# A 20-slot weight ring that first lends six slots to the attention's tensors, single buffers in the experts, and a new map for the second block

## What is computed

```python
def first_block(...):
    hn = rms_norm(h, mix_norm_g[l])
    proj = jnp.einsum('bld,dp->blp', hn, w_in[l])          # 1024 x 3072
    ...                                                    # attention and convolution
    h = h + jnp.einsum('blm,md->bld', mixed, w_out[l])     # 1024 x 1024
    h = h + expert_choice_ffn(rms_norm(h, ffn_norm_g[l]), w_router[l], w_gate[l], w_up[l], w_down[l])

def expert_choice_ffn(h, w_router, w_gate, w_up, w_down):
    ...
        logits = jnp.einsum('ld,de->le', hs, w_router, preferred_element_type=jnp.float32)
        aff = jax.nn.softmax(logits, axis=-1)
        g, idx = lax.top_k(aff.T, cap)                     # cap = 34
        xg = hs[idx]
        a = jnp.einsum('ecd,edf->ecf', xg, w_gate)         # 16 x 1024 x 2048
        u = jnp.einsum('ecd,edf->ecf', xg, w_up)           # 16 x 1024 x 2048
        y = jnp.einsum('ecf,efd->ecd', jax.nn.silu(a) * u, w_down)   # 16 x 2048 x 1024
        y = y * g[..., None].astype(y.dtype)
        out = jnp.zeros((L, D), y.dtype).at[idx.reshape(-1)].add(y.reshape(-1, D))
```

## Time and profile before

| what | value |
|---|---|
| time, median of 3 runs | 1813.72 us (1812.1 to 1817.64) |
| the profiled execution: time, span | 1817.68 us, 1815.6 us |
| PE, PEld busy | 1546.1 us (85%), 877.3 us (48%) |
| DVE, ACT, POOL busy | 570.1, 365.4, 132.9 us |
| read from memory, mean rate | 509.23 MB, 281 GB/s |

### The profile page before, as it was taken

How to read it: one execution, slowest core, us unless ns; L and a number is a source line. 1 busy time by engine, 2 the same in 40 slices (tenths; PEclk the granted TensorE clock), 3 DMA queues, 4 the chain that set the end, 5 groups by cost and what they waited for, 6 DMA issues and landing times.

```text
span 1815.6 us, 18257 instructions
## 1 busy us (share of the span) xinstructions
PE 1546.1 (85%) x7629; PEld 877.3 (48%) x7629; DVE 570.1 (31%) x982; ACT 365.4 (20%) x662; POOL 132.9 (7%) x137
## 2 busy tenths in 40 slices
PE   7989798787877877878778778699698979979999
PEld 6564433222221322222212222297587779968887
DVE  2353300100100101001001010396675564767843
ACT  1221110000000000000000000255132445445542
POOL 1000000000000000000000000101331160320000
PEclk9999799999999999999999999899898989989999
DMA  9220699999999999999999999553231324545554
GB/s 385 107 93 24 241 416 415 415 419 416 415 415 419 416 415 415 419 415 415 416 419 416 415 416 419 227 163 128 82 105 56 105 79 147 167 140 168 191 194 143
DMA packets 99665, 511.47 MB, mean 282 GB/s; under 512 B 9520, under 2 KB 9776, under 8 KB 64640
## 3 DMA queue, kind: packets, MB, share of 16 engines
q1 hardware_dynamic: 97744, 504.68, 71.2%
q10 hardware_dynamic: 1616, 3.93, 0.6%
q0 software_dynamic: 224, 1.70, 0.3%
HBM read 509.23 MB, written 1.05 MB: 281 GB/s over the span
## 4 chain that ended last, share of the span: by engine, by line
PE 45%; DMA 40%; DVE 9%; ACT 3%; POOL 2%; issue 2%; ACTq 0%; SPq 0%; DVEq 0%; POOLq 0%
DMA sb_ring<-in_w_up 23%; DMA sb_ring<-in_w_gate 15%; PE PS L703 7%; PE PS L1051 6%; PE PS L622 5%; PE PS L430 4%; PE PS L660 4%; PE PS L720 3%; PE PS L739 2%; PE PS L639 2%; PE PS L812 2%; PE PS L532 2%; PE PS L719 1%; DVE sb_wp L1837 1%; DMA sb_ring<-in_w_down 1%
## 5 line engine op out<-in xcount | busy, mean ns | idle before, releaser
L622 PE MATMUL PS<-sb_ring,sb_XG 128*64 128x512 f32 x2048 | 492.6, 606 | 124.9 <-DMA sb_ring<-in_w_up 65.9
L622 PEld LDWEIGHTS PS<-sb_ring,sb_XG 128*64 128x64 f32 x2048 | 129.2, 136 | 482.8 <-DMA sb_ring<-in_w_up 163.6
L1815 DVE TENSOR_TENSOR sb_Hh<-sb_SL,PS 128x512 f32<-128x512 f32 x32 | 20.6, 684 | 831.8 <-PE PS L622 831.8
L660 PE MATMUL PS<-sb_ring,sb_HT 128*64 128x512 f32 x1024 | 234.5, 607 | 30.8 <-DMA sb_ring<-in_w_down 16.2
L1837 DVE TENSOR_TENSOR sb_wp<-sb_raw,sb_wp 128x1024 fp32r<-128x1024 f32 x160 | 201.7, 1263 | 97.2 <-ACT sb_wp L1237 95.7
L703 PE MATMUL PS<-sb_hr,sb_wp 128*128 128x256 f32 x1440 | 190.0, 295 | 8.1 <-ACT sb_wp L1237 5.4
L1237 ACT CAST sb_wp<-sb_raw 128x1024 fp32r<-128x1024 f32 x160 | 167.0, 1046 | 128.6 <-PE PS L1051 56.1
L703 PEld LDWEIGHTS PS<-sb_hr,sb_wp 128*128 128x128 f32 x1440 | 184.7, 202 | 11.8 <-issue 8.2
L660 PEld LDWEIGHTS PS<-sb_ring,sb_HT 128*64 128x64 f32 x1024 | 80.8, 139 | 174.3 <-issue 108.1
L1214 ACT ACTIVATE sb_SL<-PS 128x512 f32<-128x512 f32 x32 | 17.4, 594 | 536.8 <-PE PS L622 536.8
L720 PE MATMUL PS<-sb_hr,sb_wp 128*128 128x512 f32 x256 | 89.9, 404 | 3.4 <-DVE sb_hr L1850 3.4
(11 more groups left out here) (387 smaller groups left out, 1242.4 us busy)
## 6 DMA issues: line engine op xcount, KB each, us to landing
sb_ring<-in_w_gate SPq DMA_DIRECT2D x128, 1024.0 KB, 24.2
sb_ring<-in_w_up SPq DMA_DIRECT2D x128, 1024.0 KB, 25.3
sb_ring<-in_w_down SPq DMA_DIRECT2D x128, 1024.0 KB, 21.0
sb_raw<-in_w SPq DMA_DIRECT2D x160, 512.0 KB, 3.6
sb_ring<-in_w_in SPq DMA_DIRECT2D x12, 1024.0 KB, 15.2
sb_ring<-in_w_out SPq DMA_DIRECT2D x4, 1024.0 KB, 10.0
sb_KW<-in_kw POOLq DMA_DIRECT2D x1, 1403.0 KB, 6.3
sb_H<-in_x ACTq DMA_DIRECT2D x2, 512.0 KB, 5.1
```

The lines of the kernel that those rows point to most:

```text
L622: ins = e.matmul(PS[64 * g:64 * g + 64, b, :], m.XG[:, k, r0:r0 + 64], m.ring[s][:, (2 * g + q) * 512:(2 * g + q) * 512 + 512], start=(k = ...
L660: ins = e.matmul(PS[64 * g:64 * g + 64, b, :], m.HT[:, ex % 2, c % 8, (c // 8) * 64:(c // 8) * 64 + 64], m.ring[s][:, a * 1024 + g * 512:a ...
```

## The change

The ring gets 20 slots. Loads 0 to 15 go through the first 14 of them; slots 14 to 19 hold tensors of the first attention until these are dead. The expert loads then go round all 20 in the order `ROUND`, in which the slots come free:

```diff
-RING = 12
+RING = 20
+IN_SLOTS = 14
+ROUND = tuple(range(2, 12)) + tuple(range(14, 20)) + (12, 13, 0, 1)
+RAW_SLOT, WP_SLOT = 6, 9
-def ring_turn(i):
-    return i % RING, i // RING + 1
+def ring_slot(i):
+    return i % IN_SLOTS if i < 16 else ROUND[(i - 16) % RING]
...
+def last_of(s):
+    last = expert_slot(NE - 1, 23)
+    return max(i for i in range(last - RING + 1, last + 1) if ring_slot(i) == s)
```

What SP waits for ahead of load i (in `sp_program`):

```diff
+    def freed(i):
+        s = ring_slot(i)
+        if i < IN_SLOTS:
+            return []
+        if i < 16:
+            return [used(i - IN_SLOTS)]
+        if i >= 16 + RING:
+            return [used(i - RING)]
+        if s < 2:
+            return [used(IN_SLOTS + s)]
+        if s < IN_SLOTS:
+            return [used(s)]
+        if s < 17:
+            return [("in", "o", 2), ("out", "conv", 11)]
+        if s < 18:
+            return [("in", "oT", 2), ("out", "conv", 11)]
+        return [("in", "wo", 1, 1), ("meta rows",)]
-        if i >= RING:
-            sp.wait_ge(*at(*used(i - RING)))
+        for event in freed(i):
+            sp.wait_ge(*at(*event))
```

**Room for it.** `aT` and `wk` of the top-k lie in `gbc`, and so ACT issues the load of the final gains only after the ranks are turned. In the experts `Y` and `HT` have one buffer, and `Hh` is gone (DVE multiplies within `SL`):

```diff
-                act.wait_ge(*at("out", "gu", ex - 1, q, 1))
+                act.wait_ge(*at("in", "ht", ex - 1, q))
...
-        if ex > 1:
-            act.wait_ge(*at("used", expert_slot(ex - 2, 23)))
-        e.copy(m.HT[:, ex % 2, 0:4, :], PS[:, b, :].rearrange("p (k c) -> p k c", k=4)).then_inc(*mark("act_moe", "out", "ht", ex, 0))
+        if ex > 0:
+            act.wait_ge(*at("used", expert_slot(ex - 1, 23)))
+        e.copy(m.HT[:, 0:4, :], PS[:, b, :].rearrange("p (k c) -> p k c", k=4)).then_inc(*mark("act_moe", "out", "ht", ex, 0))
...
-        if p > 1:
-            act.wait_ge(*at("in", "sc", p - 2, 1, 1))
+        if p > 0:
+            act.wait_ge(*at("in", "sc", p - 1, 1, 1))
```

**The second block's map.** Its tensors are laid anew: `hr` over slots 0 and 1, `raw` over 6 and 7, `KW` over 7 and 8, `wp` over 9 to 12. The first three pieces are split before the last expert's result is copied out:

```diff
 (ACT, in the loop over experts, between the copy to HT and the copies to Y)
+        if ex == NE - 1:
+            for n in range(3):
+                act.wait_ge(*at("used", last_of(WP_SLOT + n)))
+                hi(n)
...
 (ACT, after the second block's norm)
-    hi(0)
+    e.dma_start(m.SW, t["sgw"]).then_inc(*mark("ld_sgw", "sgw", by=16))
     turned("h1", m.sq)
-    hi(1)
-    hi(2)
...
 (DVE, after the last copy to HT)
+    for n in range(3):
+        lo(n)
     scattered(NE // 2 - 1)
...
-    lo(0)
     dve.wait_ge(*at("kw2"))
     turned("h1", m.VW[:, W_N1:W_N1 + 8], m.sq)
-    lo(1)
-    lo(2)
```

`KW` is loaded by SP, behind raw piece 2, and no more by POOL; `SW` by ACT:

```diff
         fetch_raw(raw_turn(n), t["w2"][n], ("lo", n))
+        if n == 2:
+            sp.wait_ge(*at("used", last_of(RAW_SLOT + 1)))
+            sp.wait_ge(*at("used", last_of(RAW_SLOT + 2)))
+            e.dma_start(m.KW, t["kw2"]).then_inc(*mark("ld_kw2", "kw2", by=16))
```

More of the change, by code:

```diff
@@ L252, in take @@
             return v
+        at[0] = ring0 + 2048 * IN_SLOTS
+        self.qraw, self.t1, self.t2 = take("qraw", 2 * L, 2), take("t1", 2 * L, 2), take("t2", 2 * L, 2)
+        self.kT = take("kT", 4 * L, 4)
+        self.qT = take("qT", 4 * L, 4)
+        self.Am, self.AT = take("Am", 2 * L, 2), take("AT", 2 * 3 * 128, 2, 3)
+        self.cv = take("cv", 2 * L, 2)
+        assert at[0] <= ring0 + 17 * 2048
+        at[0] = ring0 + 17 * 2048
+        self.O, self.up = take("O", 3 * 512, 3), take("up", 2 * (L + 2), 2)
+        self.O2 = take("O2", 3 * 512, 3)
+        self.mixT = take("mixT", 8 * L, 8)
+        ar0 = ring0 + 2048 * RING
+        assert at[0] <= ar0
+        at[0] = ar0
         self.XN = take("XN", 3072, 3)
@@ L256, in __init__ @@
         self.junk = take("junk", 1024)
-        self.qraw, self.t1, self.t2 = take("qraw", 2 * L, 2), take("t1", 2 * L, 2), take("t2", 2 * L, 2)
-        self.kT = take("kT", 4 * L, 4)
-        self.qT = take("qT", 4 * L, 4)
         self.V = take("V", 3 * 512, 3)
[L261 to L269, removed]
+        self.Pm = take("Pm", 4 * L, 2, 2)
+        self.cxs = take("cxs", L)
+        self.aT = self.gbc[:, 0:L + 6]
+        self.wk = self.gbc[:, 280:280 + 2 * (L + 6)].rearrange("p (a b) -> p a b", a=2)
         at[0] = ar0
@@ L293, in __init__ @@
         self.BH = hr.rearrange("p q (j c) -> p q j c", j=2)
-        raw0 = ring0 + WR * 2048 + 4096
-        self.raw_over = (raw0 - ring0) // 2048
+        at[0] = ring0 + 4096
+        self.R1, self.R4 = take("R1", 4096), take("R4", 4096)
+        raw0 = at[0]
+        assert raw0 == ring0 + 2048 * RAW_SLOT
         self.raw = [sb(f"raw{r}", raw0 + 1024 * r, 1024) for r in range(RAW)]
-        big0 = at[0] = raw0 + 1024 * RAW
-        self.R1, self.R4 = take("R1", 4096), take("R4", 4096)
+        at[0] = raw0 + 1024 * RAW
+        KW = take("KW", NK2 + NW2)
+        self.KW, self.KT, self.VW = KW, KW[:, 0:NK2], KW[:, NK2:NK2 + NW2]
+        at[0] = ring0 + 2048 * WP_SLOT
+        wp = sb("wp", at[0], WR * 2048, F32R).rearrange("p (w q c) -> p w q c", w=WR, q=2)
+        self.wp_hi, self.wp_lo = [wp[:, w, 0, :] for w in range(WR)], [wp[:, w, 1, :] for w in range(WR)]
+        big0 = at[0] = at[0] + WR * 2048
         self.NN = NN = take("NN", 3072)
@@ L423, in proj @@
     def proj(tile, bank, slot, half):
-        s, turn = ring_turn(slot)
+        s = ring_slot(slot)
         b = room(bank, *tile)
@@ L1199, in act_program, with hi @@
                      accum_out=m.rt[0:n, 4 * ti + 1:4 * ti + 2]).then_inc(*mark("act_out", "out", "lg", ti))
-    for ti in range(3):
-        act.wait_ge(*at("xn2", ti))
+    act.wait_ge(*at("ranks"))
+    act.wait_ge(*at("in", "ranksT"))
     e.dma_start(m.gbc, t["gbc"][1]).then_inc(*mark("ld_gbc", "gbc", 1, by=16))
+    def hi(n):
+        if n < P_END:
+            act.wait_ge(*at("raw", raw_turn(n)))
+            if n >= WR:
+                act.wait_ge(*at(*piece_done(n - WR)))
+            e.copy(m.wp_hi[n % WR], m.raw[raw_turn(n) % RAW]).then_inc(*mark("act_split", "hi", n))
     for c in range(8):
```

91 lines of the change are left out of this document (36 added, 55 removed).

## The result

The changed kernel takes 1796.18 us (median of all 4 executions) where the kernel before took 1814.39 on the same chip; the ratio is 0.9894, 95% interval 0.9872 to 0.9916. One of the four, 1855.01 us at a granted clock of 0.83 over the whole span, is left out of the ratio, and why it was slow isn't known; the other three took 1793.74, 1795.79 and 1796.57, and 1795.79 is their median. The predicted time was 1794.2, the range 1789 to 1800. The profiled execution took 1793.74 us with a span of 1791.5.

What follows compares the result with a forecast made beforehand. The experts' end was taken as set by when the unbroken weight stream starts and the loads still to come. 20.2 + 0.3 - 1.0 = 19.5 us less, from the median 1813.72 to 1794.2 us; range 1789 to 1800.

Steps and rivals of the forecast that it cites:

- The eight slots: Expert weight stream: eight more loads land before it starts at 212.43, each worth 2.526 us; 20.2 us gained, bounds 19 to 21.
- D: Stream start: at 1.2 GHz PE frees slots slower than DMA fills them; 10 us lost, 1804 us; chance 0.05.
- F: Early loads: SP's queue holds them until 212.43, or the stream doesn't end the experts; no change, 1813.7 us; chance 0.02.
- The rate: Expert stream: 415 to 419 GB/s from the trace, 2.526 us a load; the skill's 358 GB/s would give 23.4 us.
- Single buffers: Experts: new waits are for products earlier in PE's order, with 14 us of slack per expert behind; cost nothing.
- KW: Stream head: its load leaves POOL's queue at 207.25 and goes out behind raw piece 2; 0.3 us gained, bounds 0 to 0.5.
- The split ahead of the last copies to Y: Hand-over to the second block: casts make Y 2.8 us late, 1.8 us given back before PE's first product; net -1.0 us.
- rival C: Last scatter: PE stands 4.1 us, the clock falls and the 3.71 us scatter takes twice as long; 1797.9 us; chance 0.14.
- my likeliest case: Whole kernel: 19.5 us less, giving 1794.2 us, its own range 1791 to 1798; chance 0.62.
- Rival B: Last copies to Y: pieces land with load 399, casts fit into PE's last products, split costs nothing; 1791.4 us; chance 0.15.
- one of my signs of being wrong: Second block: the prediction is wrong if it takes another time than before by more than 3 us.
- E: Second block: shifted gaps hold PE at 1.2 GHz for 39 us more, costing 19.5 us; slower than before; chance 0.02.

Runs made afterwards that it cites:

- The ladder of 12, 16 and 20 loads: Changed kernel with load i from 28 waiting for i - 12 (1816.38 us), or from 32 for i - 16 (1806.64); 20 is the unedited changed kernel (1795.94).
- the dummy products: Changed kernel plus four 128x512 matmuls nobody reads on PE, between last down products and last scatter: 1795.28 us, ratio 0.9895 to the kernel before.
- the second ratio: Changed kernel measured again without edit, against the kernel before: 1795.94 us against 1815.40, ratio 0.9885 (0.9867 to 0.9904).

## Why the prediction was right, point by point

**The eight slots** (20.2 us, bounds 19 to 21): right in place, cause and size. Load 36 went out at 212.29, the pitch was 60.71 us (60.6 expected), the stretch 200 to 205 stayed nearly empty, and the stream took 20.6 us less (945.8 against 925.2). The ladder of 12, 16 and 20 loads shows it causally: 2.59 us per load by the traces (2.53 to 2.66 over all the profiles), 2.56 by the medians. That a slot is worth the transfer of one load, no more and no less, holds as long as the extra loads land before the stream starts; here they did, by some 9.5 us (202.8 to 212.29). Rivals D and F are out: with 20 slots the stream doesn't break, and with the look-ahead taken back the gain is gone.

**The rate** stayed at 416 GB/s, and the sum by the Trainium skill's 358 GB/s (DMA: Bandwidth & Descriptors, Specifications) would have been off by 3 us: the step from 12 to 20 loads measured 20.4 to 20.7 us, and 23.4 was the figure by the page. The same page's section Bandwidth has 358 GB/s for both cores of a pair streaming and measures 425 GB/s with the other core idle; one core works here, and 414 to 419 GB/s is nearer to that.

**Single buffers** (0): right, 945.4 against 945.8 us of stream. The slack behind them is nearer to 12 us per expert than to the 14 that I took: PE is idle for 143 of 737 us, which is 11.8 of 60.6.

**KW** (0.3, bounds 0 to 0.5): at the end of the stream under 0.1 us. The lower bound was the better value. In its new place it took 18.0 us from issue (1126.63) to landing, so 1144.6, 7.1 us behind the start of the last down products (7.2 to 8.7 expected) and 13.4 ahead of the turned rows at 1157.97. The issues of `gbc` and `SW` held ACT for 0.33 and 0.34 us, less than half a us each as expected.

**The split ahead of the last copies to Y** (net -1.0): this is the term that was mis-sized. From PE's end to the first product of the second block it is 23.9 us, where 22.4 was expected; at the conv loop's second tile the part costs 1.5 us (32.0 against 30.5 before) and not 1.0. Its working had three parts. `Y` late by 2.8 us: measured 2.9 (a cast takes 1.05 us; the 0.94 that I took was only the part of it that stood in the chain). Given back 1.8: the profile with the dummy products, whose clock stayed up in the wait, is the clean measure. Against the split left in its old place it is 0.9 us behind at PE's first product (22.5 and 21.6) and 0.6 at the conv loop (31.2 and 30.6). So 2.0 us are given back at the one and 2.3 at the other, and the clock behind the first product has a share in the second. The third part, the clock, was left out of the sum and put into rival C. It fell in each profile that has the late `Y` and no dummy products (5.10, 5.11, 5.15 and 6.47 us for a scatter of 3.7). In the changed kernel it cost 1.4 us in the scatter, of which 0.8 is left at the conv loop, and not C's 3.7, because the clock fell near the end of the wait and came back within the scatter. So my likeliest case and C each held in part. C's reading that the clock falls after some 5 us without work was a single case: here it fell 3.6 us after PE's end. Rival B is out: the pieces land behind load 399, at a spacing of 1.3 us.

**Luck in the sum.** That the sum is so near is in part luck, for three misses nearly cancel: PE's last down products came 20.75 us earlier where 20.2 was the term, `KW` gave nothing where 0.3 was the term, and the split cost 0.5 more than its 1.0.

**The accounting of the profiles.** Down to the second tile of the conv loop: 20.75 - 1.5 = 19.3 us (1190.71 to 1171.45), the prediction's sum of 19.5 within 0.3. Between the profiles a further 4.8 us lie in the second block, which I had counted as unchanged; a difference there of more than 3 us was one of my signs of being wrong, and the profiles show that sign. 4.5 of them arise in one stretch: products that started at 1374.89 before start at 1354.86 after (20.0 us less), later ones at 1424.21 and 1399.69 (24.5). Of the kernel before, a window there:

```profile
1385.00:1390.00 5.00, 5.00 (x18) 3.02 (x19) 0.69 (x1) 1.26 (x2) 0.00 (x0) 0.50 0.00 0
```

and from its timeline the first taps of that tile and the products in that window:

```profile
1190.71 0.36 DVE L1888 TENSOR_SCALAR sb_R<-sb_R,sb_KW 128x256 f32<-128x256 f32 x1
...
1388.63 4.76 PE L703 MATMUL PS<-sb_hr,sb_wp 128*128 128x256 f32 x24
```

And of the changed kernel, the same products and their window:

```profile
1365.83 3.13 PE L726 MATMUL PS<-sb_hr,sb_wp 128*128 128x256 f32 x24
```

```profile
1365.00:1370.00 5.00, 4.98 (x38) 4.16 (x36) 2.68 (x4) 1.91 (x3) 0.40 (x1) 1.00 0.05 7
```

The clock stood at 0.50 there from 1382.1 to 1392.3 in the profiled execution of before and not in that of after. Over the whole rest of the second block the kernel before ran 10 us longer at 0.50, so this is E's mechanism at a quarter of the 39 us that decide, and with the other sign.

It is no accident of one execution. The stretch from that tile to the end of the span takes 620.1 us in both profiles of the changed kernel, 620.2 to 620.9 with the look-ahead of 16 and 12 and with the split behind `Y`, but 624.3 with the dummy products, 625.9 with the split left in its old place, 624.8 in the kernel before and with `KW` early, 626.1 with single buffers. PE's program of this part is the same in all; where the clock falls in it is not. What makes it fall differently stays open. Whether the executions that weren't profiled have the 4.8 us isn't known either. Their medians differ by 18.2 and 19.5 us, near the 19.3 at the conv loop, so most of it doesn't show there; but the interval of the second ratio (0.9867 to 0.9904) reaches to 24 us. Had I judged the steps by the two profiled times (23.9 us), I would have looked for 4 us of gain in the ring and the hand-over, where it isn't.

## What to carry to other kernels

Where a stream of transfers is the bound from its start to the end of a stage, its end moves by (loads more in hand when the unbroken stream starts) x (time of one load), as long as the engines use a load faster than it comes; so borrow memory that is dead only until then, and count the slots. Work placed ahead of a copy on an in-order engine can cost the wait for its own input, and not only its duration: put it behind the copy and it fills the wait that the copy opens. A wait of a few microseconds on PE can cost its own length and a slower clock behind it, so price both, and compare the parts of two profiles, not their totals, when a few microseconds are at stake.

## What the runs showed of the hardware that I had not expected

- A wait of PE of 4.14 or 4.15 us stretched the scatter behind it from 3.70 us to 5.10, 5.11, 5.15 or 6.47: the same wait, different costs, as the low stretch of the clock began earlier or later and lasted 3.4 or 6.8 us. With a wait of 0.52 us (dummy products) or 1.28 us the clock stayed at 1.00.
- How soon the clock falls after PE stops varies too. Behind the last scatter it took 5.3 us before the change, but 2.1 us with single buffers (PE stops at 1160.85, the clock is at 0.95 in 1162 to 1163 and at 0.50 in the next microsecond) and 2.0 us with the split left in its old place. In the wait for `Y` it took 2.9 us (look-ahead of 12) to 3.7.
- The attention, whose program is the same in all profiles of the kernel before and its variants, took up to 4 us more or less: the first waiting load went out at 212.43, 212.44 and 208.54.
- The second block from the second tile of the conv loop on, with the same program on PE, took 620.1 to 626.1 us from profile to profile, as the clock fell in other places.
